# Delta rule: the first problems' decays, keys and first inversion moved between the last tiles of the value projection, and the last joining of each inversion begun one step earlier

## The reference

```
qkv = silu(short_conv(p[..., :DN_QKV_DIM], conv_w))       # 4096 columns, 5 taps along the tokens
q, k = l2_normalize(q) * 128 ** -0.5, l2_normalize(k)     # 8 heads of 128
v = 16 heads of 128;  g = -exp(a_log) * softplus(a + dt_bias);  beta = sigmoid(b)
for each direction (forward, backward), chunk by chunk:
    gcum  = cumsum(g);  decay = exp(gcum_i - gcum_j) below the diagonal
    m     = strictly lower part of beta_i * (k_i . k_j) * decay
    u, w  = solve (I + m) x = [v * beta, k * beta * exp(gcum)]
    v_new = u - w @ s
    o     = (q * exp(gcum)) @ s + ((q . k) * decay) @ v_new
    s     = s * exp(gcum_last) + (k * tail)^T @ v_new
```

## Time and profile before

| | us |
|---|---|
| median of three timed runs | 3067.75 |
| profiled execution, its own time | 3072.86 |
| its span | 3071.1 |
| last four tiles of the projection, 1411.9 to 1542.9 | 131.0 |
| from there to the first joining product, 1542.9 to 1602.5 | 59.6 |
| step -1 and step 0, 1602.5 to 1642.9 | 40.4 |
| steps 1 to 15, 1642.9 to 1946.5 | 303.6 |
| everything behind | 1124.5 |

### The profile page before, as it was taken

How to read it: one execution, slowest core, us unless ns; L and a number is a source line. 1 busy time by engine, 2 the same in 40 slices (tenths; PEclk the granted TensorE clock), 3 DMA queues, 4 the chain that set the end, 5 groups by cost and what they waited for, 6 DMA issues and landing times.

```text
span 3071.1 us, 37490 instructions
## 1 busy us (share of the span) xinstructions
PE 2887.0 (94%) x14521; PEld 2238.0 (73%) x14521; DVE 1361.7 (44%) x2257; ACT 694.2 (23%) x1384; POOL 655.1 (21%) x513
## 2 busy tenths in 40 slices
PE   7999999999899999999957888999999999998999
PEld 3565488888666888644447888778688886697888
DVE  2236378762225333255447665665455122233100
ACT  1134121110223221143234554330100002321100
POOL 1000055453100000000033442444355440020000
PEclk8999999999999999999969999999999999999999
DMA  7447222222416444443232332222122223111343
GB/s 286 170 163 266 82 84 95 83 96 94 147 69 240 179 154 145 176 160 142 111 76 62 80 71 50 105 69 83 69 96 83 83 96 128 55 42 67 139 151 110
DMA packets 108331, 357.42 MB, mean 116 GB/s; under 512 B 41200, under 2 KB 60400, under 8 KB 69136
## 3 DMA queue, kind: packets, MB, share of 16 engines
q1 hardware_dynamic: 86432, 334.65, 31.0%
q10 hardware_dynamic: 20160, 15.40, 1.6%
q0 software_dynamic: 1584, 5.21, 0.5%
HBM read 344.62 MB, written 10.62 MB: 116 GB/s over the span
## 4 chain that ended last, share of the span: by engine, by line
PE 75%; issue 10%; DVE 5%; DMA 4%; ACT 3%; DVEq 1%; POOL 1%; SPq 0%; ACTq 0%; POOLq 0%
PE psum L2794 29%; PE psum L233 22%; PE psum L358 3%; PE psum L267 3%; PE psum L663 3%; PE psum L2350 2%; PE psum L493 1%; PE psum L520 1%; DMA inv_d<-vec 1%; DMA ring<-in_stream 1%; DMA ring<-gsums 1%; PE psum L1556 1%; ACT h_sb L1048 1%; PE psum L505 1%; PE psum L2451 1%
## 5 line engine op out<-in xcount | busy, mean ns | idle before, releaser
L233 PE MATMUL psum<-h_sb,ring 128*128 128x256 f32 (+1 forms) x2400 | 729.7, 465 | 18.8 <-ACT h_sb L1048 16.1
L233 PEld LDWEIGHTS psum<-h_sb,ring 128*128 128x128 f32 x2400 | 456.8, 192 | 279.6 <-issue 223.8
L2794 PE MATMUL psum<-arena,ring 128*128 128x256 f32 x1688 | 383.2, 379 | 0.2 <-DVE arena L2857 0.2
L2794 PEld LDWEIGHTS psum<-arena,ring 128*128 128x128 f32 x1688 | 320.6, 190 | 44.2 <-DVE arena L2857 0.6
L2794 PE MATMUL psum<-arena,c 128*128 128x256 f32 x1080 | 249.0, 379 | 0.0
L233 PE MATMUL psum<-arena,ring 128*128 128x256 f32 x992 | 220.9, 387 | 9.4 <-DVE arena L1018 4.7
L2794 PEld LDWEIGHTS psum<-arena,c 128*128 128x128 f32 x1080 | 205.1, 190 | 29.7 <-issue 1.9
L233 PEld LDWEIGHTS psum<-arena,ring 128*128 128x128 f32 x992 | 192.5, 194 | 37.8 <-DVE arena L1018 5.1
L1956 POOL TENSOR_TENSOR ring<-ring,c 128x512 f32<-128x512 f32 x28 | 35.8, 1302 | 788.6 <-DMA ring<-gsums 788.6
L2809 POOL TENSOR_TENSOR rows<-ring 128x512 f32<-128x512 f32 (+1 forms) x39 | 52.9, 1356 | 556.1 <-DVE arena L2837 336.5
L2794 PE MATMUL psum<-h_sb,ring 128*128 128x256 f32 x688 | 155.7, 379 | 8.6 <-DVE kst L2873 8.6
(11 more groups left out here) (346 smaller groups left out, 4182.2 us busy)
## 6 DMA issues: line engine op xcount, KB each, us to landing
ring<-in_stream SPq DMA_DIRECT2D x302, 1024.0 KB, 4.8
ring<-gsums SPq DMA_DIRECT2D x28, 256.0 KB, 4.8
arena<-decays SPq DMA_DIRECT2D x24, 256.0 KB, 4.9
keys_d<-kst ACTq DMA_DIRECT2D x16, 256.0 KB, 2.8
x_sb<-in_x ACTq DMA_DIRECT2D x1, 2048.0 KB, 19.2
arena<-in_rpb POOLq DMA_DIRECT2D x32, 64.0 KB, 8.2
keys_d<-c ACTq DMA_DIRECT2D x7, 256.0 KB, 3.2
keys_d<-silu_w ACTq DMA_DIRECT2D x6, 256.0 KB, 3.0
```

Of the source, the lines that this page charges most:

```text
L233: ins = pe.matmul(out_ap, lhs(k), rhs(k), start=first and k == 0, stop=last and k == nk - 1)
L2794: ins = pe.matmul(dst, self.seven_weights(n, i, k, nk), self.seven_moving(x, sums, i, k, nk), start=first and j == 0 and k == 0, stop=last ...
```

## The change

1. `EARLY = 4`: problems 0 to 3 are prepared during the projection. The loop then runs from s = -1 on TensorE, ScalarE, VectorE and GpSimd, and the first inversion is done in the last pair of tiles.
2. The tiles that this needs lie where value heads already turned have lain (`area(8192...)`): SP waits for the count of copied heads (`v_copied`) before each `sum_rows`. The score tiles of these problems lie in `LT`.
3. The keys of these problems use banks 5 and 6, so value heads turn through bank 4 alone, and each turn waits for the copy of the one before.
4. SP's weight loads are cut in pieces between the new waits.
5. In the loop, side 0 of the 16 x 16 joining stands at the end of the odd step, ahead of `dve_state_next`, and side 1 with `dve_inverse_out` ahead of `dve_right` of level 4 in the even step.

```diff
+EARLY = LEAD - 1
@@ views
-        self.AT = [[ring[:, at + 512 * d:at + 512 * d + 512] for d in range(2)] for at in (0, 1024, 2048, 3072, 6144)]
-        self.AT.append([area(14336 + 512 * d, 512) for d in range(2)])
-        self.DT = [ring[:, at:at + 1024] for at in (7168, 4096, 5120)]
+        early = [area(at, 1024) for at in (8192, 10240, 11264, 12288, 13312)]
+        later = [ring[:, at:at + 1024] for at in (6144, 0, 1024, 2048, 3072)] + [area(14336, 1024)]
+        tiles = early + [later[x % 6] for x in range(DELTA_STEPS - LEAD)]
+        self.AT = [[tile[:, 0:512], tile[:, 512:1024]] for tile in tiles]
+        self.DT = [area(9216, 1024)] + [ring[:, (7168, 4096, 5120)[x % 3]:][:, 0:1024] for x in range(1, DELTA_STEPS)]
+        self.KQ = [[self.LT[:, 256 * d:256 * (d + 1)] if x < EARLY else area(15872 + 256 * d, 256) for d in range(2)]
+                   for x in range(DELTA_STEPS)]
@@ pe_qkv, pe_turn_v
+            if rho == 28:
+                self.pe_turn_keys(pe, 1)
-        if hv >= 3:
-            pe.wait_ge(T["v_copied"], hv - 2)
+        if hv > 0:
+            pe.wait_ge(T["v_copied"], hv)
@@ pe_between (act_between alike)
+        if (j, half) == (7, 1):
+            self.pe_turn_keys(pe, 2)
         if j >= 5:
-            for hv in range(2):
-                self.pe_turn_v(pe, 4 * (j - 5) + 2 * half + hv)
+            first = 4 * (j - 5) + 2 * half
+            self.pe_turn_v(pe, first)
+            if (j, half) == (6, 0):
+                self.pe_turn_keys(pe, 0)
+            self.pe_turn_v(pe, first + 1)
+        early = {(5, 1): 0, (6, 1): 1, (7, 0): 2, (7, 1): 3}.get((j, half))
+        if early is not None:
+            if early == 0:
+                pe.wait_ge(T["l_done"], 1)
+            for d in range(2):
+                self.pe_keys(pe, early, d)
@@ pe_delta
-        pe.wait_ge(T["l_done"], 1)
+        self.pe_turn_keys(pe, 3)
-        for s in range(-LEAD, DELTA_STEPS):
+        for s in range(-1, DELTA_STEPS):
@@ sp_delta (inverses(m): the old block of waits, stores and loads)
+        loads(RING, behind(3))
         sp.wait_ge(T["decays_out"], 1)
...
         sp.wait_ge(T["decays_out"], 33)
-        sp.wait_ge(T["qkv_ready"], QKV_CHUNKS // 2 + 1)
-        sp.wait_ge(self.b["S"]["products"], 2 * self.b["sched"]["2z"][0])
-        for x in range(LEAD):
...
+        loads(behind(3), behind(10))
+        sp.wait_ge(T["v_copied"], 2)
+        sum_rows(0)
+        loads(behind(10), behind(12))
+        sp.wait_ge(T["v_copied"], 6)
+        sum_rows(1)
+        self.sp_blocks_in(sp, 0)
+        loads(behind(12), behind(13))
+        sp.wait_ge(T["v_copied"], 8)
+        sum_rows(2)
+        loads(behind(13), z0)
+        self.sp_blocks_in(sp, 1)
+        sp.wait_ge(T["v_copied"], 10)
+        sum_rows(3)
+        sp.wait_ge(T["v_copied"], 12)
+        sum_rows(4)
+        self.sp_blocks_in(sp, 2)
+        sp.wait_ge(self.b["S"]["products"], 2 * z0)
+        inverses(0)
@@ act_delta, last pair
+                if (j, q) == (7, 0):
+                    self.act_turned_keys(act, 1)
+                    self.act_keys_out(act, 1)
...
+        self.act_turned_keys(act, 3)
+        self.act_keys_out(act, 3)
@@ pool_delta
+        for x in range(EARLY):
+            self.pool_bars(pool, x)
+            for d in range(2):
+                self.pool_scores(pool, x, d)
+        self.pool_inverse(pool, 0)
@@ dve_delta, projection
+                if (j, q) == (7, 1):
+                    self.dve_inverse_fours(dve, 0)
+                    for d in range(2):
+                        self.dve_keys(dve, 2, d)
+                if (j, q) == (7, 2):
+                    self.dve_inverse_eights(dve, 0)
+                    self.dve_inverse_side(dve, 0, 8, (0,), 0)
             dve.drain().then_inc(T["tapped"], 1)
+            if j == 7:
+                self.dve_inverse_side(dve, 0, 8, (0,), 1)
+                self.dve_inverse_out(dve, 0)
+            if j >= 5:
+                for d in range(2):
+                    self.dve_keys(dve, (0, 1, 3)[j - 5], d)
@@ dve_delta, steps
+            if last is not None:
+                self.dve_inverse_side(dve, last, 8, (0,), 1)
+                self.dve_inverse_out(dve, last)
             if a is not None:
                 self.dve_right(dve, a, 4)
-            if last is not None:
-                self.dve_inverse_side(dve, last, 8, (0,), 0)
...
             if a is not None:
                 self.dve_left(dve, a, 6)
+            if m is not None:
+                self.dve_inverse_side(dve, m, 8, (0,), 0)
             if c is not None and c < 3:
                 self.dve_state_next(dve, s, 0)
```

143 lines of the change are left out of this document (82 added, 61 removed).

## The result

The changed kernel took 3020.6 us (median of four runs, 3015.99 to 3022.86), the kernel before on the same chip 3070.28. The ratio is 0.9832, 95% interval 0.9808 to 0.9856: 1.7% faster, 49.7 us. I had forecast 3012 us. The same kernel ran in two later comparisons too: 3014.94 us at a ratio of 0.9825 [0.9799, 0.9851], and 3014.06 at 0.9828 [0.9804, 0.9853]. One kernel's runs lie up to 20 us apart. The profiles show some of this outside the changed stretch: in the fourteen profiles of this case the first value turn, up to which the engines' work is the same, began anywhere between 1450.2 and 1463.0 us, and what follows the delta rule took between 1123.5 and 1133.1 us. So small terms are read here from the lengths of stages within a trace.

What follows compares the result with a forecast made beforehand. TensorE bounds the projection's end and even steps; chains of waits bound the warm-up and odd steps. Gains 31.4 + 25.2 = 56.6 us; 3072.9 - 56.6 - 5.1 (profiled execution to median) = 3011.2, so 3012 us; 8-in-10 range 3000 to 3034.

Steps and rivals of the forecast that it cites:

- Projection: Moving four problems into the projection makes its last weight product end 10.0 us later on TensorE.
- the single bank: In the projection, a pair's second value head waits for ScalarE's copy of the first: 0.85 us, five pairs, 4.3 us.
- Rival C: SP's waits before weight loads outlast the ring of four and prefetch is lost: 90 us, 3102 us; chance 0.03.
- Tail: From the last weight product to the first joining product: 19.3 us instead of 60.7, so 41.4 us saved.
- B: End of the projection's last weight product, at 1541.8 us before the change and forecast at 1551.8.
- the rule: VectorE instructions with two SBUF inputs and GpSimd's SBUF reads exclude each other; 2.5 us in the tail, left out.
- Rivals B and D: B: tail handoffs cost more, 12 to 15 us, 3025, chance 0.09. D: first inversion still last, 3032, chance 0.05.
- Odd steps: In steps 1, 3, 5, 7, 9 decays start at +4.1 us instead of 9.0: 24.5 us gained.
- the three transitions: Steps 1, 5 and 9 into the next: first half delays VectorE's state updates, 1.7 us each, 5.1 us cost.
- part 2: Last joining begun in the odd step: 24.5 + 7.0 - 6.3 = 25.2 us gained.
- Rival A's first condition: Sums' load for odd steps lands 3 us later; with full state-update costs 3035 us; whole rival's chance 0.17.
- The 0.7 us a pair: Moving the joining's second half away from GpSimd's scores gives 0.7 us a pair, some 5 in all; left out.

Runs made afterwards that it cites:

- the second profile: Profile of the changed kernel run again unaltered, on the same chip as the two parts: 3014.94 us, ratio 0.9825.
- part 1 alone: Changed kernel with both sides of the 16 x 16 joining back in their old place, four problems still prepared in the projection: 3040.9 us, ratio 0.991.
- both edits: Changed kernel with GpSimd's two score products of problem 3 behind its spreading of the first inverse, and value heads 13 and 15 through bank 6: 3011.55 us.

## Why the prediction was right, point by point

The terms against the stages (steps from the second profile, where no fall of the clock disturbs):

- **Projection.** 10.0 forecast, 10.3 measured. Of it the single bank was 4.3 by the forecast and 3.7 by the run with two banks throughout, so the keys' products and turns were some 6.5 and not 5.7. No engine's queue made TensorE wait but ScalarE's copies, and no wait for the weights' ring shows. Rival C (SP's holds) did not happen; what a hold that is too long would cost was not tried.
- **Tail.** From B to the first joining product 19.3 forecast, 20.9 measured, so 39.8 us saved and not 41.4. The step that failed is the one that left out the port shared by VectorE and GpSimd: the first value turned at B + 14.6 instead of + 13.0, and with GpSimd's scores out of the way at + 12.7. The prediction's estimate by the rule was 2.5 us in the tail; 1.9 were measured. The rule stood beside the sum and was the better guide. Rivals B and D are out.
- **Odd steps.** The decays begin at + 3.81 (forecast + 4.1). Steps 3 and 7 with the even steps behind them: 9.4 forecast, 9.7 measured (11.4 gained in steps 3 and 7, 1.7 lost in steps 4 and 8, where the forecast had 0.4 lost and less gained; neither run that moved or dropped a half changed steps 4 and 8, so the cause of that loss is open). Steps 11 and 13: 6.8 forecast, 8.8 measured. 5.3 of it is waiting that went away, and 3.5 is TensorE busy a shorter time with the same instructions.
- **The clock in the steps.** The forecast put nothing for it. It took 4.9 us of waiting from each of five odd steps, from the decays of step 1, which had no fall of the clock. The falls in steps 3, 7, 9, 11 and 13 went with the waits, and TensorE's busy time fell by 2.0, 2.9, 1.8, 1.7 and 1.8 us there. Since steps 3, 7, 11 and 13 came out above their terms by this and the three transitions below theirs, part 2's sum (25.2 forecast; 25.8 measured in steps 1 to 15, less 1.0 lost in steps -1 and 0) was met in part by luck.
- **The two waits of the odd step.** The 4.9 us were read from the decays alone. The trace of before has two waits, one behind the other: in step 1 the first joining product waits 2.28 us for the inverse (3.12 in step 3), and later TensorE waits 0.94 and 1.37 us for GpSimd and ScalarE, behind the late decays. Both went with part 2, and no run parts them.
- **The three transitions.** Steps 1, 5 and 9 with 2, 6 and 10: 9.6 forecast, 7.2 measured. The term that was mis-sized is their cost. The forecast took 1.7 us each for all of it; the first half alone cost that, at the end of the odd steps (21.8, not 19.5 to 20), and the second half ahead of the joining sum another 0.6 on average in the even ones (20.0, not 20.5 to 21). That is 1.8 of the missing 2.4 us. The other 0.6 is in the waits: without the first half the three odd steps were 14.1 us shorter than before (2.0 of it TensorE's shorter busy time in step 9), against 3 x 4.9 = 14.7. Rival A's first condition, a late load of sums, did not come: the decays begin at + 3.81.
- **The 0.7 us a pair** that the rule about the shared port would give back for the second half did come (L2298 at 1636.48 takes 1.03 us, 1.73 before), but the first half now meets GpSimd's scores (L2036, from 1626.94 to 1628.22) and takes 1.56 instead of 1.04. The collision has moved to the costlier place. Leaving this pair of terms out of the sum was right by luck.
- **Steps -1 and 0:** 0.6 forecast, 1.0 measured.

In the profiles the stretch of the change is 52.4 us shorter in the first and 54.4 in the second, against 56.6 forecast. The two profiled executions are 56.9 us apart, but 5.1 of that lies ahead of the first value turn, where the change does nothing: that this agrees with 56.6 is chance. The measured 49.7 between the medians of four runs has an interval of 44 to 59 us, in which 56.6 lies, and the two later comparisons put 56.0 and 53.9 between the medians. The 5.1 us that I took off for the median stood on three runs; in all comparisons the medians of the kernel before were from 3067.7 to 3071.0, so 2 to 5 below its profiled execution. The sum gave 3011.2, and the forecast was written down as 3012.

## What to carry to other kernels

A chain of waits in which every engine is under half busy can be moved beside a full engine at the price of its instructions there: here 10 us bought 40. When a stall is removed by work put elsewhere on an engine that has no room there, price both ends: here the decays came 5.2 us earlier and the step only 3.5, and the run without that work got 5.2. Look at the granted clock of the stage as well: where a wait goes away, a fall of the clock behind it can go too, here up to 2.9 us in one step. And where VectorE and GpSimd both work on SBUF on the path, look at which of them starts first in each pair, since a copy of 128x4 elements can cost 1.2 us.

## What the runs showed of the hardware

- VectorE and GpSimd hold each other up in small and plain operations too: a VectorE copy of 128x4 fp32 took 0.17 us alone and 1.22 beside GpSimd's product, a product of 128x512 took 1.04 alone and 1.56 to 1.73, one of 128x2048 2.29 and 3.19, and GpSimd's own, of 128x512, 1.27 and 2.17. A VectorE operation with one input in PSUM kept its length: the state update (L2354) took 1.12 us at 1629.95 and 1.12 at 1631.59, where all of it ran beside GpSimd's work (1630.38 to 1632.89).
- The same idle time of TensorE (1.85 and 1.87 us at the same instruction of step 4) was followed by a lower granted clock in one execution and not in the other, 0.9 us a step. In the odd steps of the kernel before and of the one with part 1 alone, TensorE's waits of 3.1 to 3.3 us for the inverse all had a fall in or behind them; of the waits of 1.8 to 2.5 us five had one and three had none.
- Behind idle time, with sixteen turns in a row (3.4 to 3.7 us, four profiles), the clock was back at 2.4 GHz between 0.4 us before and 0.8 us behind the start of the next product; with the same turns one by one, 0.68 us apart, 3.4 us behind it in the changed kernel. It did not always stay: in three of the four the 40 us that follow were 1.8 us shorter, and in the kernel with both edits, where a wait of 1.56 us came first, the clock fell again for 10.2 us.
